# Softmax pieces: exponential straight from PSUM, output copies on ACT, residue moves on SP, another spread of the sample chunks

## The reference

```
s = einsum(q, k) / sqrt(64);  s = where(mask, s, -1e30)
m = max(s);  e = exp(s - m);  den = sum(e);  o = (e @ v) / den;  lse = m + log(den)
...  # samples: the same over 129 gathered keys of a cache and the new keys
out = sum over the three groups of softmax(lse) * o        # combined by log-sum-exp
```

## Time and profile before

| | |
|---|---|
| median of 3 runs | 1187.04 us |
| the profiled execution | 1189.63 us, of which the span of the instructions 1187.7 us |
| PE busy / DVE / ACT / POOL | 1086.7 / 704.1 / 395.4 / 290.7 us |
| granted clock over the span | 0.965 of full speed |
| transfers, share of the 16 DMA engines' time | hardware queues 35.3% and 2.4%, POOL's software queue 13.8% |

### The profile page before, as it was taken

One profiled execution on the slowest core, in us unless ns is written; L12 is line 12 of the kernel. 1 busy time (PEld: TensorE's weight loads), 2 busy tenths in 40 slices (PEclk: granted clock), 3 DMA queues, 4 the chain that ended last, 5 costly groups with the idle time before them and its releaser, 6 DMA issues.

```text
span 1187.7 us, 20928 instructions
## 1 busy us (share of the span) xinstructions
PE 1086.7 (91%) x8478; PEld 1063.0 (90%) x8478; DVE 704.1 (59%) x847; ACT 395.4 (33%) x611; POOL 290.7 (24%) x427
## 2 busy tenths in 40 slices
PE   4888999897999869887679999999999999999997
PEld 4888899897999769887679998999999999999996
DVE  4347877885868876998563635444343434344553
ACT  4332243332432334314223545331331232143422
POOL 2785367408672001100000021010100101011300
PEclk9998999998999989888879999999999999999999
DMA  6635645577358734355547223556564656555422
GB/s 180 196 104 184 215 146 168 190 216 210 117 186 262 206 137 141 105 162 162 158 143 236 90 72 107 186 168 207 164 196 163 205 173 194 175 197 176 158 72 76
DMA packets 129662, 196.14 MB, mean 165 GB/s; under 512 B 28720, under 2 KB 104976, under 8 KB 127792
## 3 DMA queue, kind: packets, MB, share of 16 engines
q1 hardware_dynamic: 111120, 131.38, 35.3%
q0 software_dynamic: 4096, 55.22, 13.8%
q10 hardware_dynamic: 14368, 8.46, 2.4%
HBM read 186.07 MB, written 62.00 MB: 209 GB/s over the span
## 4 chain that ended last, share of the span: by engine, by line
PE 55%; DVE 15%; POOL 12%; issue 6%; SPq 5%; DMA 4%; ACT 3%; ACTq 0%; DVEq 0%; POOLq 0%
PE gm L999 48%; SPq L489 4%; POOL st L1711 3%; POOL fin L1747 3%; DVE w_lo L1270 3%; DVE kv L1418 2%; DVE acc L1426 2%; DVE kv L1377 2%; DMA w_raw<-in_w_in 2%; ACT w_hi L599 1%; DVE sq L1290 1%; POOL rot L1755 1%; DMA out_kvp<-V 1%; PE gm L975 1%; POOL fin L1758 1%
## 5 line engine op out<-in xcount | busy, mean ns | idle before, releaser
L999 PE MATMUL gm<-h_hi,w_hi 128*128 128x272 f32 x1088 | 232.0, 295 | 14.7 <-DVE z L1303 7.6
L1270 DVE TENSOR_TENSOR w_lo<-w_raw,w_hi 128x1024 fp32r<-128x1024 f32 x150 | 179.6, 1237 | 87.0 <-ACT w_hi L599 85.2
L999 PE MATMUL gm<-h_hi,w_lo 128*128 128x272 f32 x1088 | 228.0, 291 | 0.0
L999 PE MATMUL gm<-h_lo,w_hi 128*128 128x272 f32 x1088 | 227.2, 291 | 0.0
L599 ACT CAST w_hi<-w_raw 128x1024 fp32r<-128x1024 f32 x150 | 149.7, 1044 | 151.9 <-PE gm L999 116.6
L975 PE MATMUL gm<-w_hi,h_hi 128*128 128x256 f32 x640 | 192.0, 300 | 6.0 <-issue 6.0
L999 PEld LDWEIGHTS gm<-h_hi,w_hi 128*128 128x128 f32 x1088 | 173.9, 192 | 15.9 <-issue 15.3
L976 PE MATMUL gm<-w_hi,h_lo 128*128 128x256 f32 x640 | 184.5, 288 | 0.0
L977 PE MATMUL gm<-w_lo,h_hi 128*128 128x256 f32 x640 | 183.8, 287 | 0.0
L999 PEld LDWEIGHTS gm<-h_lo,w_hi 128*128 128x128 f32 x1088 | 174.1, 192 | 0.0
L999 PEld LDWEIGHTS gm<-h_hi,w_lo 128*128 128x128 f32 x1088 | 172.7, 192 | 0.0
(11 more groups left out here) (246 smaller groups left out, 1473.1 us busy)
## 6 DMA issues: line engine op xcount, KB each, us to landing
w_raw<-in_w_ff SPq DMA_DIRECT2D x64, 512.0 KB, 5.1
out_kvs<-in_cache_kv_w POOLq DMA_DIRECT2D x64, 510.0 KB, 4.1
w_raw<-in_w_in SPq DMA_DIRECT2D x60, 512.0 KB, 5.8
kv<-in_cache_kv_w SPq DMA_DIRECT2D x128, 128.0 KB
kv<-in_cache_kv_w SPq DMA_DIRECT2D x64, 256.0 KB
out_kvs<-in_cache_kv_w POOLq DMA_DIRECT2D x32, 508.0 KB, 4.7
kv<-in_cache_kv_w SPq DMA_DIRECT2D x128, 64.0 KB
w_raw<-in_w_o SPq DMA_DIRECT2D x8, 512.0 KB, 4.4
```

The lines of the kernel that those rows point to most:

```text
L999: last = nc.tensor.matmul(gm[:, 2 * b2 + half, 0:HALF], w, x[:, k0 + k, half * HALF:(half + 1) * HALF], start=first, stop=end)
L1270: vec.tensor_tensor(w_lo[:, r, cols], w_raw[:, hh], w_hi[:, r, cols].bitcast(F32), ALU.subtract).then_inc(w_lo_done, 1)
```

## The change

- DVE keeps only the maximum of a piece, and writes it, times minus the scale, to a small tile `ngm` (128x4 or 128x2). ACT computes the exponential straight out of `psS`, with `ngm` as its per-row bias: two instructions of 256 columns in group 0, four of 128 in groups 1 and 2. `psS` is free for the next piece when these are done (`exp_done`), and DVE's next maximum waits for the exponentials of two pieces before.
- The copies of a piece's output from `psO` into `O` go from the end of DVE's slot to the end of ACT's slot.
- The 16 residue DMAs go from POOL's slot 37 to SP's slot 40.
- `CHUNKS_AT` is new. In the slots 9 to 47 the q and k panels take 1, 2, 0 chunks and the v panels 1, 2, 1. Behind them slots 54 to 59 take 7 chunks (8 before), 60 to 72 take 10 (12 before), 73 to 79 take 10 (9 before), and 80 to 83 take 8 (6 before). The last keys chunk of group 2 goes from slot 75 to 78, so `m1`, `m2`, `ds` go to slots 79, 81, 83, and the last values chunk goes from 82 to 83.
- Code for chunks on POOL that no slot used is gone.

```diff
--- before.py
+++ after.py
@@ -106,26 +106,13 @@
         CHUNKS += [(_kind, _g, _j, 2) for _j in range(0, KEYS[_g], 2)] + [(_kind, _g, KEYS[_g], 1)]
...
-    CHUNKS_AT[_s] = 1
...
-for _s, _n in zip(range(55, 60), (2, 1, 2, 2, 1)):
-    CHUNKS_AT[_s] = _n
-for _s in (60, 61, 62, 63, 64, 65, 66, 67, 68):
-    CHUNKS_AT[_s] = 1
-for _s, _n in zip(range(70, 76), (1, 1, 1, 2, 2, 2)):
-    CHUNKS_AT[_s] = _n
-for _s, _n in zip(range(77, 83), (1, 1, 1, 2, 2, 2)):
+SPREAD = (1, 2, 0, 1, 2, 1, 1, 1, 1, 0, 1, 1, 1, 0, 1, 0, 1, 1, 1, 2, 2, 2, 1, 1, 1, 1, 2, 2, 2, 2)
+CHUNKS_AT = {}
+for _s in list(range(9, 48, 3)):
+    CHUNKS_AT[_s], CHUNKS_AT[_s + 1], CHUNKS_AT[_s + 2] = 1, 2, int(UNITS[_s][1] == "v")
+for _s in (48, 51):
+    CHUNKS_AT[_s], CHUNKS_AT[_s + 1], CHUNKS_AT[_s + 2] = 1, 2, 1
+for _s, _n in zip(range(54, 84), SPREAD):
     CHUNKS_AT[_s] = _n
 CH_SLOT = [_s for _s in sorted(CHUNKS_AT) for _ in range(CHUNKS_AT[_s])]
 assert len(CH_SLOT) == NCH, (len(CH_SLOT), NCH)
@@ -143,9 +130,6 @@
...
@@ -329,6 +313,7 @@
+        ngm = sb("ngm", [128, 2, 4], F32, A_K + 7424)
...
@@ -534,6 +518,11 @@
                 for n in range(RING, NCH):
                     if s == CH_SLOT[n - RING] + 3:
                         load_chunk(n)
+                if s == 40:
+                    sp.wait_ge(o_out, 16)
+                    for a in range(4):
+                        for b in range(4):
+                            sp.dma_start(O0[32 * b:32 * b + 32, a], O_blk[a:128:4, b]).then_inc(o_moved, 16)
                 if s in V_BACK:
                     g = V_BACK[s]
...
@@ -779,6 +768,21 @@
+            def take_output(j):
+
+                g, hd, pair = PIECES[j]
+                O = (O_blk, O1, O2)[g]
+                act.wait_ge(pv_ready, j + 1)
+                if j == 24:
+                    act.wait_ge(o_moved, 256)
+                    act.wait_ge(t_ready, TINDEX[("ws",)] + 1)
+                W = HD + 1
+                if g:
+                    dst, n = O[:, :, hd, 0:W], 4
+                else:
+                    dst, n = O[:, 2 * pair:2 * pair + 2, hd, 0:W], 2
+                nc.scalar.copy(dst, psO[:, 0:W * n].rearrange("p (a d) -> p a d", d=W)).then_inc(o_out, 1)
...
@@ -851,8 +855,16 @@
                 if s in S_AT:
                     j = S_AT[s]
-                    act.wait_ge(s_used, SINDEX[("piece", j)] + 1)
-                    nc.scalar.activation(prob[:, j % 2], prob[:, j % 2], ACT.Exp, scale=SCALE).then_inc(exp_done, 1)
+                    act.wait_ge(max_ready, j + 1)
+                    if j >= 2:
+                        act.wait_ge(t_ready, TINDEX[("pt", j - 2)] + 1)
+                    w = 128 if PIECES[j][0] else 256
+                    for x in range(512 // w):
+                        e = nc.scalar.activation(prob[:, j % 2, w * x:w * x + w], psS[:, w * x:w * x + w], ACT.Exp, scale=SCALE,
+                                                 bias=ngm[:, j % 2, x:x + 1])
+                    e.then_inc(exp_done, 1)
+                if s - 2 in S_AT:
+                    take_output(S_AT[s - 2])
...
@@ -1128,7 +1140,7 @@
             def scores(job):
                 n = SINDEX[job]
                 if n >= 1:
-                    pe.wait_ge(s_used, n)
...
@@ -1340,27 +1352,13 @@
                     dve.wait_ge(o_moved, 256)
                     dve.wait_ge(t_ready, TINDEX[("ws",)] + 1)
                 if j >= 2:
-                    dve.wait_ge(t_ready, TINDEX[("pt", j - 2)] + 1)
+                    dve.wait_ge(exp_done, j - 1)
                 if g:
-                    m, sv, pv = O[:, :, hd, 65], psS[:].rearrange("p (a n) -> p a n", a=4), prob[:, j % 2].rearrange("p (a n) -> p a n", a=4)
-                    w = 128
+                    m, sv, w = O[:, :, hd, 65], psS[:].rearrange("p (a n) -> p a n", a=4), 128
                 else:
-                    m, sv = O[:, 2 * pair:2 * pair + 2, hd, 65], psS[:].rearrange("p (a n) -> p a n", a=2)
-                    pv = prob[:, j % 2].rearrange("p (a n) -> p a n", a=2)
-                    w = 256
+                    m, sv, w = O[:, 2 * pair:2 * pair + 2, hd, 65], psS[:].rearrange("p (a n) -> p a n", a=2), 256
                 link(vec.tensor_reduce(m, sv, AX.X, ALU.max))
-                vec.tensor_tensor(pv, sv, bc(m, 2, w), ALU.subtract).then_inc(s_used, 1)
-            def take_output(j):
-                g, hd, pair = PIECES[j]
-                O = (O_blk, O1, O2)[g]
-                dve.wait_ge(pv_ready, j + 1)
-                W = HD + 1
-                if g:
-                    dst, n = O[:, :, hd, 0:W], 4
-                else:
-                    dst, n = O[:, 2 * pair:2 * pair + 2, hd, 0:W], 2
-                vec.tensor_copy(dst, psO[:, 0:W * n].rearrange("p (a d) -> p a d", d=W)).then_inc(o_out, 1)
-
+                vec.tensor_scalar(ngm[:, j % 2, 0:512 // w], m, -SCALE, None, ALU.mult).then_inc(max_ready, 1)
...
@@ -1642,8 +1635,6 @@
                     gained_lo(0, sub)
                 for job in SJOBS.get(s, []):
                     take_scores(job)
-                if s - 2 in S_AT:
-                    take_output(S_AT[s - 2])
...
@@ -1815,11 +1783,6 @@
-                if s == 37:
-                    pool.wait_ge(o_out, 16)
-                    for a in range(4):
-                        for b in range(4):
-                            pool.dma_start(O0[32 * b:32 * b + 32, a], O_blk[a:128:4, b]).then_inc(o_moved, 16)
```

More of the change, by code:

```diff
@@ L143, in kind_count @@
     return sum(1 for c in CHUNKS[:n + 1] if c[0] == CHUNKS[n][0])
-POOL_KEYS = [n for n, c in enumerate(CHUNKS) if c[0] == "keys" and (48 <= CH_SLOT[n] < 54 or CH_SLOT[n] >= 62)]
-POOL_VALUES = [n for n, c in enumerate(CHUNKS) if c[0] == "values" and (30 <= CH_SLOT[n] < 36 or CH_SLOT[n] >= 54)]
-POOL_KEYS, POOL_VALUES = [], []
 SLOTS = U_FF
@@ L1371, in take_keys @@
                 c = kv[:, n % RING, 0:nk]
-                if n in POOL_KEYS:
-                    dve.wait_ge(keys_scaled, POOL_KEYS.index(n) + 1)
-                else:
-                    dve.wait_ge(chunk_landed[n % RING], chunk_count(n))
-                    dve.wait_ge(q_landed, 16 * T * (g + 1))
-                    link(vec.tensor_tensor(c, c, bc(Qb[:], 1, nk), ALU.mult))
+                dve.wait_ge(chunk_landed[n % RING], chunk_count(n))
+                dve.wait_ge(q_landed, 16 * T * (g + 1))
+                link(vec.tensor_tensor(c, c, bc(Qb[:], 1, nk), ALU.mult))
                 vec.tensor_reduce(sc[:, j:j + nk], heads(c), AX.X, ALU.add).then_inc(keys_used, 1)
@@ L1420, in take_values @@
                     out.then_inc(values_used, 1)
-                elif n in POOL_VALUES:
-                    out.then_inc(values_scaled, 1)
                 else:
@@ L1804, in _ @@
                     finish_heads(s - 1)
-                for n in CH_AT.get(s, []):
-                    if n in POOL_VALUES:
-                        add_values(n)
-                for n in CH_AT.get(s + 1, []):
-                    if n in POOL_KEYS:
-                        scale_keys(n)
                 if kind in ("k", "q"):
```

29 lines of the change are left out of this document (2 added, 27 removed).

## The result

| | before | changed |
|---|---|---|
| median of 17 runs each, us | 1188.8 (1186.6 to 1193.7) | 1195.6 (1191.6 to 1201.6) |
| profiled execution, span, us | 1187.7 | 1196.8 |
| busy us: PE, DVE, ACT, POOL | 1086.7, 704.1, 395.4, 290.7 | 1088.7, 679.2, 414.4, 287.2 |
| mean granted clock | 0.965 | 0.961 |

The ratio of the runs is 1.0057, 95% interval 1.0042 to 1.0073. The changed kernel is slower by 0.6%, 6.8 us, where 1169 us was forecast, with 1153 as the low and 1183 as the high end. DVE lost 24.9 us of work and ACT gained 19 (27 and 25 were forecast), so the change does what it says. The traces are of one execution each: the changed one took 1198.4 us, 2.8 above its median, and the one before 1189.6, 0.9 above. So the differences between the traces sum to 9.1 us, and not to 6.8. One run of e4 took 2097.5 us at a granted clock of 1.00 and is left out of its figures.

The account below looks back on a forecast made before the run. The loss was taken to be PE's idle time and lower clock ahead of 606 us. Terms -4 -10 -5 -4 +5.5 = -17.5 us from the profiled 1189.6, with medians 2.6 below, gave 1169 us; range 1153 to 1183.

Parts of the forecast that it names:

- The stretch 122.6 to 252.5 us: Group 1's heads with group 0's pieces: 4 of PE's 5.9 us idle behind a full DVE go; bounds 0 and 5.9.
- The start to unit 18: The kernel up to 122.6 us, ahead of group 0's pieces: no change, 0 us.
- The residue moves: Around unit 40: without POOL's 8.67 us of issues PE's wait of 5.54 goes; 10 us faster, bounds 5 and 11.
- The va units: 374 to 431.2 us: one chunk less and two lighter pieces on DVE, plus clock; 5 us faster, bounds 0 and 14.9 + 2.9.
- 431.2 to 505.9 us: PE's wait at 484.27 shrinks as a chunk and an output copy leave DVE; 4 us faster, bounds 0 and 8.
- The relief of DVE: From slot 57's split to unit 59's join DVE works 15.2 us, before 19.5; 27 us less busy in all.
- 505.9 us to the end of gb: `ds` waits for slot 83 behind SP's issues; 5.5 us slower, bounds 3 us faster and 26 us slower.
- The rival of the slower side: End of the samples: SP at 1.0 us per issue delays `ds`, 26 us more than taken, median 1195; chance 0.09.
- The exponential: ACT's instructions per piece: about 1.1 us for four of 128 columns, 0.8 for two of 256.
- The one for being wrong by way of `psS`: Sign that the forecast is wrong: PE's waits for `psS` grow, with ACT as releaser.
- 0.88 for faster: Summed chance of the first four cases: forecast 0.56, paid in full 0.17, SP in the middle 0.12, `psS` 0.03.
- four gains: The terms -4 (122.6 to 252.5 us), -10 (residue moves), -5 (va units) and -4 (431.2 to 505.9 us).

Follow-up runs that it names:

- e4: The changed kernel with the old `CHUNKS_AT` from slot 54 on, the new one before it; 1191.2 us, 1.0010.
- e13: The changed kernel with the next group's queries loaded five slots after a group's last keys, not three; 1195.5 us, 1.0045.
- e14: The changed kernel with one chunk moved from slot 13 to slot 20; 1197.1 us, 1.0055.
- e2: The changed kernel with the old `CHUNKS_AT` for all slots; work on ACT and moves on SP stay; 1183.9 us, 0.9944.
- e1: The kernel before with only the 16 residue moves going from POOL's slot 37 to SP's slot 40; 1181.9 us, 0.9942.
- e6: The kernel before with the moves on SP and the new `CHUNKS_AT`, none of the work moved to ACT; 1194.8 us, 1.0049.
- e10: e2 with every second chunk of group 2 issued by POOL; 1171.4 us, 0.9850.
- e7: e1 with every second chunk of group 2 issued by POOL; 1170.7 us, 0.9840.
- e17: e15 without the work on ACT: subtraction, exponential out of SBUF and copies as in the kernel before; 1159.2 us, 0.9733.
- e15: e8 with the edits of e13 and e14; 1163.1 us, 0.9779.
- e8: The changed kernel with every second chunk of group 2 issued by POOL; 1167.8 us, 0.9812.

## Why the prediction was wrong

*The stretch 122.6 to 252.5 us, -4 (measured +7.9).* This is the step that failed. "Nothing else here is late, so I take 4 us; bounds 0 and 5.9" left out any loss. I had priced the table by how many chunks it takes from DVE around a wait of PE, and not by what it moves elsewhere: the slot of the queries hangs on the last keys, and the table took that load two slots forward on a queue that issues in order, with weights behind it (e13). Before, the same wait was there with 6.5 us, so it could be read. The ninth chunk in slots 12 to 18 (e14) could be counted from the order; the prediction spoke of these slots nowhere. All in all the table, counted as a gain, costs 13.5 us (the changed kernel against e2).

*The start to unit 18, 0 (measured +2.3).* 1.0 us is the pair in slot 10. 1.1 us stand already at unit 1, where the runs of kernels with the same code differ by up to 1.6.

*The residue moves, -10 (measured -10.0).* Right in place and, in the traces, in size; e1 alone gives 6.9 us in the timed runs. PE has no idle time over 0.4 us in units 40 to 47, so SP's moves held nothing up there, as costed.

*The va units, -5, and 431.2 to 505.9 us, -4 (measured +1.4 and -0.8).* The relief of DVE came as forecast: from the end of the split of slot 57 (411.75 + 2.36) to the end of the join of unit 59 (429.11 + 0.41) there are now 15.4 us, where the prediction had 15.2 and the kernel before has 19.5.

```profile
411.75 2.36 DVE L1282 TENSOR_TENSOR w_lo<-w_raw,w_hi 128x1024 fp32r<-128x1024 f32 x2 [4.78 <-ACT w_hi L588]
429.11 0.41 DVE L1315 TENSOR_TENSOR z<-gm,sq 32x256 f32<-32x256 f32 x1
```

But the split itself, which the prediction held at 411.5, ends 2.6 us later, at 414.1, so that PE's unit 60 starts only 1.5 us earlier. The weights left SP 0.7 us sooner than before (399.05, 399.74). Before, ACT's cast waited for them (407.54). Now it starts at 410.67, directly behind the exponential and the output copy in ACT's stream, and these stood behind waits for PE; without the work on ACT (e6) it starts at 409.15. What failed here is the path: the moved work stands ahead of the cast that DVE waits for, which by e6 is 1.5 us of the 2.6.

The wait for `psS` of unit 56, 8.43 us and 1.9 before, had no place in the prediction. It is there in e1 too (5.6), which has the old table and the old arithmetic but whose PE arrives 11 us earlier. DVE comes to the maximum of slot 54 only 7.7 us earlier there (382.07, before 389.75): from the split of slot 48 on it stands still only in two waits, 4.6 us of 37, and the rest is its own work, mostly the chunks of slots 48 to 53, of which both tables have eight. So once POOL's stall is gone this work of DVE is what PE meets, and the new table adds the 2.4 us of its chunk in slot 54. No run with fewer chunks in slots 48 to 53 was made, so this part is read from the traces and not shown by an edit.

The idea behind both terms, that a lighter DVE pays where DVE is at 87% of the time, failed in e2 against e1, e10 against e7 and e15 against e17. The page of the profile shows where the 24.9 us went. The splits of weights, before and changed (busy us, mean ns, idle time ahead of them and what ended it):

```profile
L1270 DVE TENSOR_TENSOR w_lo<-w_raw,w_hi 128x1024 fp32r<-128x1024 f32 x150 | 179.6, 1237 | 87.0 <-ACT w_hi L599 85.2
```

```profile
L1282 DVE TENSOR_TENSOR w_lo<-w_raw,w_hi 128x1024 fp32r<-128x1024 f32 x150 | 178.8, 1231 | 113.9 <-ACT w_hi L588 112.1
```

DVE waits 27 us longer for ACT's casts, as much as it was relieved of. A busy share of 87% was no proof that DVE's own work ended the waits.

*505.9 us to the end of gb, +5.5 (measured +9.7).* The mechanism was right: `ds` waits in unit 84, behind slot 83's chunks, and SP's queue has no gap (e8). Mis-sized by 4 us: I had the denominators done at about 624 with 505.9 held, and DVE's step came at 628.2, which is 628.7 on that scale, since the stretch starts 0.5 us earlier now. The first weights left SP at 589.43 and the last chunk at 622.8, 33.3 us where I had 31 (part of the issues took 0.72 us and not 0.64), and from there to DVE's step it was 5.4 us and not 4. The rival of the slower side had this place, but with 1.0 us per issue; the issues stayed at 0.63 to 0.72. Its time, 1195, came out by another way, so that it was met by luck.

*The exponential.* Four of 128 columns were taken at 1.1 us and two of 256 at 0.8. They took 1.14 (from 395.46) and 0.85 us:

```profile
198.60 0.85 ACT L863 ACTIVATE prob<-psS,ngm 128x256 f32<-128x256 f32 x2
```

The Trainium skill (ScalarE: Activation LUTs, "What ACT_TABLE_LOAD costs") gave 1.27 and 0.89 by estimate; the trace lies between those and mine, and neither decides anything, since e6 has the same waits without it.

*The signs.* The one for being wrong by way of `psS` (longer waits, ACT as releaser) came true as it was worded, but e6 shows that its mechanism was not at work. The waits in the earlier trace rows have six causes and not five, and POOL is busy 69% of the stretch around its stall and not four fifths; neither moves the sum.

*The chances.* 0.88 for faster rested on four gains, three bounded at 0 and one at 5. Two of them turned out losses; a table that moves 86 chunks over 75 slots should have had a bound below nothing for each stretch.
